# A three-layer transformer forward pass on one core: the opening norm's scales by pairs of units, its shifts as narrow matmuls

## The chip, the cores and the metric

The kernel runs on one core of a Trainium2 chip. The metric is the device time of one execution in microseconds, lower is better. The core has TensorE (PE; its weight loads are listed apart as PEld and overlap the matmuls), VectorE (DVE), ScalarE (ACT), GpSimdE (POOL), SyncE (SP, which issues nearly all DMAs) and 16 DMA engines between HBM and the on-chip memory. Engines run their own instructions strictly in order and wait for each other on semaphores.

## The reference

All arrays are float32. A first block has two layers, a second block one; the tokens are 256 rows of 1024. What the change touches is the start of layer 0 of the first block: the modulation vector, the first RMS norm and the first projection.

```python
def rms_norm(x, g):
    xf = x.astype(jnp.float32)
    y = xf * lax.rsqrt(jnp.mean(xf * xf, axis=-1, keepdims=True) + EPS)
    return (y * g.astype(jnp.float32)).astype(x.dtype)

def hybrid_layer(x, mod, norm1, norm2, w_in, ...):
    shift1, scale1, gate1, shift2, scale2, gate2 = jnp.split(mod[:, None, :], 6, axis=-1)
    h = rms_norm(x, norm1) * (1.0 + scale1) + shift1
    proj = h @ w_in
    ...

def first_block(x, c, w_mod, b_mod, ...):
    c_act = jax.nn.silu(c)
    for l in range(DEPTH):
        mod = c_act @ w_mod[l] + b_mod[l]
        x = hybrid_layer(x, mod, ...)
    return x
```

## The kernel before

**Layout.** Activations are kept transposed: 128 features on the partitions, 256 tokens along the row, eight such blocks (kc = 0 to 7) for the 1024 features. Weights come from HBM as panels of 1 MB (128 partitions x 2048 float32; 256 output columns of a 1024-row matrix, laid out by kc). To keep float32 accuracy with the fast format, each panel and each activation is split in a high and a low part: ACT copies the panel to the high part (`split_hi`, L430), DVE subtracts it from the panel to get the low part (`split_lo`, L437), and TensorE multiplies three products per block (high x high L442, high x low L443, low x high L444). A panel is 48 such matmuls of 256 columns. Raw panels live in a ring of six slots (`raw`, the low part is written over them as `ring_w`), high parts in four (`w_hi`).

**The modulation vector.** `mod` is a vector times a matrix. Its 6144 outputs per layer are 24 units of 256 outputs, 1 MB each, with the outputs on the partitions and the 1024 inputs along the row. DVE multiplies each half of a unit with the row `crow` (silu of c, spread over all partitions by TensorE transposes) and sums along the row: `dve_mod`, L1167, two instructions a unit, each with a small one that fetches the sum. In layer 0 the units 0 to 3 are shift1 and 4 to 7 are scale1. The remaining units come later, between other work, through two buffers `modw` and the semaphore `mod_used`, on which SP waits before it reloads a buffer (L367).

**The opening.** SP issues, in this order: ccol (c, norm1 and the first 16 columns of b_mod), the first part of the constants, x (1 MB), the eight units 0 to 7 (L2333), panels 0 and 1 (L362), the rest of the constants, panels 2 to 5, and then units 8, 9 and panels 6, 7 as their buffers come free. TensorE turns c (L2374) and x (L2381), ACT copies x and squares it, TensorE sums the squares (L592), and ACT takes the inverse root `rs` (L942, L943). DVE sums the eight units, adds the bias (L1176), forms the gain `gcol` = (1 + scale) x norm1 (L2417), and then per block kc: `tbuf` = x * gcol * rs (L1195), ACT adds the shift and rounds (`act_hi`, L967), DVE takes the rest (`act_lo`, L1200). Between them stand the splits of panels 0 and 1. TensorE multiplies panel 0 (`pe_head_late`): for kc 0 to 3 first the two products with the high weights (L528, L529), then those with the low weights (L533), then kc 4 to 7 as three products. Panels 1, 2, 3 follow through `pe_panel`; the small compression matmuls (`cmp`, 60 columns) are mixed into panel 3 and need `tb`, which ACT and DVE prepare from the results of panels 0 and 1 (L999 to L1017 on ACT, L1300 and L1303 on DVE). GpSimd loads the layer's constants `lc` (436 KB) once `mod_used` stands at 2 + 7.

Everything in the rest of the program is ordered by hand in each engine's own program and by semaphores; the change leaves the order there as it is.

Of the kernel before, what the change touches and what calls it, by code (L numbers as in the profile page):

```python
# [104 lines left out]
def build(nc, a, out, layers=DEPTH):  # L105
    ctx = ExitStack()

    def sb(name, shape, dt=F32):
        return ctx.enter_context(nc.sbuf_tensor(name, shape, dt))

    def sem(name):
        return ctx.enter_context(nc.semaphore(name))

    with ctx:
# [23 lines left out]
        crow = sb("crow", [P, D])  # L138
        modc = sb("modc", [P, 48])
# [38 lines left out]
        cst_more = sem("cst_more")  # L178
        gcol_ready = sem("gcol_ready")
# [16 lines left out]
        modraw_x = [sem(f"modraw_x{i}") for i in range(6)]  # L196
# [33 lines left out]
        class Chain:  # L230
# [13 lines left out]
            def end(self):  # L244
# [33 lines left out]
        first_units = [modw[:, 0, :], modw[:, 1, :], modw_x[:, 0, :], modw_x[:, 1, :],  # L278
                       *[v[:, b * PANEL:(b + 1) * PANEL] for v in (mixf, act_flat) for b in range(2)]]
# [238 lines left out]
        def pe_head_late(pe, m, k, o, arrive):  # L518


            pe.wait_ge(hi_done, rounded(m, k))
            wh, wl = w_hi[slot(k)], w_lo(m, k)
            col = lambda kc, c: slice(kc * 256 + c * P, kc * 256 + (c + 1) * P)
            row = lambda c: o[:, c * T:(c + 1) * T]
            for kc in range(4):
                arrive(kc)
                for c in range(2):
                    nc.tensor.matmul(row(c), wh[:, col(kc, c)], act_hi[:, kc, :], start=kc == 0 and c == 0, stop=False, skip_group_check=True)  # L528
                    nc.tensor.matmul(row(c), wh[:, col(kc, c)], act_lo[:, kc, :], start=False, stop=False, skip_group_check=True)  # L529
            pe.wait_ge(lo_done, rounded(m, k))  # L530
            for kc in range(4):
                for c in range(2):
                    nc.tensor.matmul(row(c), wl[:, col(kc, c)], act_hi[:, kc, :], start=False, stop=False, skip_group_check=True)  # L533
            for kc in range(4, KC):
                arrive(kc)
                for c in range(2):
                    last = mm3(row(c), wh[:, col(kc, c)], wl[:, col(kc, c)], act_hi[:, kc, :], act_lo[:, kc, :], False, kc == KC - 1, skip=True)
            return last
# [421 lines left out]
        def act_norm(act, l, q, link, shift):  # L960
            act.wait_ge(ss_done, q + 1)
            rsqrt(link, rs[:, :], bank[6][:, 0:T], 1.0 / D, cst[:, C_EPS:C_EPS + 1]).then_inc(rs_done, 1)
            if q == 0:
                split_hi(act, 0, 0)
            for kc in range(KC):
                act.wait_ge(t_done, 8 * q + kc + 1)
                nc.scalar.activation(act_hi[:, kc, :], tbuf[:, kc, :], ACT.Identity, bias=modc[:, shift + kc:shift + kc + 1])\  # L967
                    .then_inc(act_his, 1)
                if q == 0 and kc == 3:
                    split_hi(act, 0, 1)  # L970
            if q == 0:
                act_masks(act)
# [217 lines left out]
        def dve_norm(dve, q, g0, shift):  # L1190

            dve.wait_ge(rs_done, q + 1)
            for kc in range(KC + 1):
                if kc < KC:
                    nc.vector.scalar_tensor_tensor(tbuf[:, kc, :], x[:, kc, :], gcol[:, g0 + kc:g0 + kc + 1], rs[:, :], ALU.mult, ALU.mult)\  # L1195
                        .then_inc(t_done, 1)
                if kc:
                    c = kc - 1
                    dve.wait_ge(act_his, 8 * q + c + 1)
                    nc.vector.scalar_tensor_tensor(act_lo[:, c, :], tbuf[:, c, :], modc[:, shift + c:shift + c + 1],  # L1200
                                                   act_hi[:, c, :].bitcast(F32), ALU.add, ALU.subtract).then_inc(act_ready, 1)
                    if q == 0 and c == 3:
                        split_lo(dve, 0, 0)
            if q == 0:
                split_lo(dve, 0, 1)

        def dve_layer(dve, l, link, ahead):
# [83 lines left out]
            if l:  # L1291
                dve_modc(dve, modc_ready, 3 * l + 2, 64, lc[:, LC_BM:LC_BM + 8], 36)
# [70 lines left out]
            if l == 0:  # L1363
                dve_modc(dve, modc_ready, 3 * l + 2, 16, lc[:, LC_BM:LC_BM + 8], 12)
# [999 lines left out]
        def _(pe):  # L2364
            pe.sem_inc(split_free, SPLIT)
            pe.sem_inc(mod_used, 2)
# [42 lines left out]
        def _(dve):  # L2409
            link = Chain(dve, dve_links, DVE_LINKS)  # L2410
            dve.wait_ge(cact_ready, 2)
            for u in range(8):
                dve.wait_ge(modraw[u] if u < 2 else modraw_x[u - 2], 16)
                dve_mod(first_units[u], modsum, 2 * u)
            dve.wait_ge(c_loaded, 16)
            dve_modc(dve, modc_ready, 1, 0, ccol[:, 2 * KC:2 * KC + 16], 8)
            nc.vector.scalar_tensor_tensor(gcol[:, 0:KC], modc[:, 8:16], 1.0, ccol[:, KC:2 * KC], ALU.add, ALU.mult).then_inc(gcol_ready, 1)  # L2417
            dve.wait_ge(gcol_ready, 1)
# [31 lines left out]
def lay_out(i):  # L2450
# [24 lines left out]
    modw = i["w_mod"].transpose(0, 2, 1).reshape(DEPTH * MOD_PANELS, 2, P, D).transpose(0, 2, 1, 3).reshape(-1, P, PANEL)  # L2475
    w = i["w_in_2"]
# [38 lines left out]
```

## Time and profile before

| | us |
|---|---|
| median of 3 runs (1230.19 to 1238.47) | 1230.28 |
| the profiled execution | 1229.85 |
| its span, first to last instruction | 1228.1 |
| TensorE busy in it | 1166.4 (95%) |
| DVE busy | 903.4 (74%) |
| ACT busy | 609.2 (50%) |

The profiled execution took 1.75 us more than its span. TensorE's clock was granted at 0.984 of full on the mean: it has two levels, 2.4 GHz (1.00 in the rows) and 1.2 GHz (0.50). "Idle before, releaser" is how long an engine had stood still and what let it go on.

### The profile page before, as it was taken

To read this page: it belongs to the slowest core of one execution; us is meant where nothing else is said; L and a number is where in the kernel's file an instruction comes from. 1 tells how busy PE (TensorE), PEld (TensorE's weight loads), DVE (VectorE), ACT (ScalarE), POOL (GpSimd) and SP (SyncE) were. 2 spreads that over 40 slices of the span, in tenths; PEclk is the share of its full clock that TensorE was granted. 3 is DMA by queue.
4 is the path that set the end of the run, shared out by engine and by line. 5 is a ranking of instruction groups with operands and counts; after the bars stand their busy time and mean duration, and the time that the engine had idled before them with its cause. 6 is when DMAs were issued, how large, how long until landed. Compare 5 with 4: busy or idle time off the path is not lost.

```text
span 1228.1 us, 19648 instructions
## 1 busy us (share of the span) xinstructions
PE 1166.4 (95%) x7990; PEld 1058.5 (86%) x7990; DVE 903.4 (74%) x1201; ACT 609.2 (50%) x811; POOL 58.5 (5%) x61
## 2 busy tenths in 40 slices
PE   3999999999989999999999999999999998999996
PEld 2978989999988888999999989988878997888885
DVE  6889798877788976855568369986785857656555
ACT  3753354444465435444444435557788733444441
POOL 1017000000000520000000000000000000000000
PEclk7899999999999999999999999999999999999999
DMA  9845467868765416455566534454784564555540
GB/s 379 348 170 206 169 244 282 301 244 300 276 230 231 168 52 238 172 193 184 179 248 215 175 134 138 140 193 161 245 292 138 189 219 141 171 188 190 196 146 34
DMA packets 44058, 249.34 MB, mean 203 GB/s; under 512 B 4352, under 2 KB 12672, under 8 KB 15952
## 3 DMA queue, kind: packets, MB, share of 16 engines
q1 hardware_dynamic: 43568, 246.19, 55.8%
q0 software_dynamic: 416, 2.11, 0.5%
q8 instruction: 53, 0.87, 0.3%
q14 instruction: 21, 0.17, 0.1%
HBM read 247.17 MB, written 1.11 MB: 202 GB/s over the span
## 4 chain that ended last, share of the span: by engine, by line
PE 82%; DVE 8%; ACT 5%; DMA 2%; issue 1%; SPq 0%; POOL 0%; DVEq 0%; ACTq 0%; POOLq 0%
PE bank L442 17%; PE bank L443 16%; PE bank L444 16%; PE bank L799 14%; PE bank L802 7%; PE bank L882 2%; DMA raw<-in_panels 2%; PE bank L923 1%; DVE ring_w L437 1%; ACT mixf L1953 1%; PE bank L1725 1%; PE bank L1843 1%; PE bank L781 1%; ACT mixf L1954 1%; DMA arena<-in_modw 1%
## 5 line engine op out<-in xcount | busy, mean ns | idle before, releaser
L437 DVE TENSOR_TENSOR ring_w<-raw,w_hi 128x2048 fp32r<-128x2048 f32 x166 | 381.4, 2301 | 138.8 <-ACT w_hi L430 138.5
L430 ACT ACTIVATE w_hi<-raw 128x2048 fp32r<-128x2048 f32 x166 | 316.3, 1909 | 165.3 <-PE bank L444 152.6
L442 PE MATMUL bank<-act,w_hi 128*128 128x256 f32 x728 | 211.7, 291 | 6.4 <-DVE act L1200 2.7
L443 PE MATMUL bank<-act,w_hi 128*128 128x256 f32 x728 | 206.4, 284 | 0.0
L444 PE MATMUL bank<-act,ring_w 128*128 128x256 f32 x728 | 206.3, 283 | 0.0
L799 PE MATMUL bank<-act,w_hi 128*128 128x512 f32 x736 | 184.7, 393 | 0.2 <-DVE act L2280 0.2
L443 PE MATMUL bank<-ff_lo,w_hi 128*128 128x256 f32 (+1 forms) x560 | 158.2, 283 | 0.0
L444 PE MATMUL bank<-ff_hi,ring_w 128*128 128x256 f32 (+1 forms) x560 | 158.2, 282 | 0.0
L442 PE MATMUL bank<-ff_hi,w_hi 128*128 128x256 f32 (+1 forms) x560 | 157.7, 282 | 0.0
L799 PEld LDWEIGHTS bank<-act,w_hi 128*128 128x128 f32 x736 | 133.8, 189 | 25.3 <-issue 0.6
L442 PEld LDWEIGHTS bank<-act,w_hi 128*128 128x128 f32 x728 | 140.1, 192 | 13.0 <-issue 10.0
L443 PEld LDWEIGHTS bank<-act,w_hi 128*128 128x128 f32 x728 | 140.1, 192 | 0.1
L444 PEld LDWEIGHTS bank<-act,ring_w 128*128 128x128 f32 x728 | 140.0, 192 | 0.0
L1167 DVE CUSTOM_DVE_ANT_0 arena<-arena,crow 128x1024 f32<-128x1024 f32 x88 | 106.0, 1243 | 10.8 <-DMA arena<-in_modw 10.6
L1127 ACT ACTIVATE arena<-bank 128x256 f32<-128x256 f32 x96 | 36.6, 383 | 152.8 <-PE bank L802 149.1
L443 PEld LDWEIGHTS bank<-ff_lo,w_hi 128*128 128x128 f32 x560 | 107.5, 192 | 0.0
L442 PEld LDWEIGHTS bank<-ff_hi,w_hi 128*128 128x128 f32 x560 | 107.5, 192 | 0.0
L444 PEld LDWEIGHTS bank<-ff_hi,ring_w 128*128 128x128 f32 x560 | 107.5, 192 | 0.0
L802 PEld LDWEIGHTS bank<-act,ring_w 128*128 128x128 f32 x736 | 100.4, 190 | 7.2
L802 PE MATMUL bank<-act,ring_w 128*128 128x256 f32 x736 | 102.6, 282 | 0.0
L1459 DVE TENSOR_TENSOR arena<-bank,arena 128x256 f32<-128x256 f32 x96 | 39.8, 421 | 63.3 <-ACT arena L1127 63.2
L442 PE MATMUL bank<-mix_hi,w_hi 128*128 128x256 f32 x192 | 55.4, 289 | 0.0
(347 smaller groups left out, 1887.3 us busy)
## 6 DMA issues: line engine op xcount, KB each, us to landing
raw<-in_panels SPq DMA_DIRECT2D x170, 1024.0 KB, 4.8
arena<-in_modw SPq DMA_DIRECT2D x44, 1024.0 KB, 7.2
mixf<-dscr SPq DMA_DIRECT2D x8, 512.0 KB, 5.2
arena<-dscr SPq DMA_DIRECT2D x8, 512.0 KB, 4.9
mixf<-in_modw SPq DMA_DIRECT2D x2, 1024.0 KB, 16.3
act_flat<-in_modw SPq DMA_DIRECT2D x2, 1024.0 KB, 20.0
mixf<-dscr SPq DMA_DIRECT2D x8, 256.0 KB, 6.7
arena<-dscr SPq DMA_DIRECT2D x8, 256.0 KB, 5.9
```

The source lines that it names most:

```text
L430: nc.scalar.activation(w_hi[slot(k)][:, :], w_raw(m, k), ACT.Copy).then_inc(hi_done, 1)
L437: nc.vector.tensor_tensor(w_lo(m, k), w_raw(m, k), w_hi[slot(k)][:, :].bitcast(F32), ALU.subtract).then_inc(lo_done, 1)
L442: nc.tensor.matmul(o, wh, xh, start=start, stop=False, skip_group_check=skip)
L443: nc.tensor.matmul(o, wh, xl, start=False, stop=False, skip_group_check=skip)
L444: return nc.tensor.matmul(o, wl, xh, start=False, stop=stop, skip_group_check=skip)
L781: nc.tensor.matmul(bank[c][:, :], wh[:, s:s + P], act2[:, kc, :, :], start=kc == 0, stop=False, skip_group_check=True)
L799: nc.tensor.matmul(bank[4 + c][:, :], wh[:, s:s + P], act2[:, kc, :, :], start=kc == 0, stop=False)
L802: last = nc.tensor.matmul(bank[4 + c][:, 0:T], wl[:, s:s + P], act_hi[:, kc, :], start=False, stop=kc == KC - 1)
L882: mm = lambda o, w, x, first=False, last=False: nc.tensor.matmul(o, w, x, start=first, stop=last, skip_group_check=True)
L1127: nc.scalar.activation(fr[par][:, c * T:(c + 1) * T], up_bank(at, c, final)[:, T:2 * T], ACT.Copy).then_inc(ff_cross, 1)
L1167: last = nc.vector.tensor_tensor_reduce(o, o, crow[:, :], 1.0, 0.0, ALU.mult, ALU.add, sums[:, col + b:col + b + 1])
L1459: nc.vector.tensor_tensor(fr[par][:, c * T:(c + 1) * T], up_bank(at, c, final)[:, 0:T], fr[par][:, c * T:(c + 1) * T], ALU.add).then_inc(f ...
```

## The change

The order of the opening's loads changes: scale and shift units alternate (4, 0, 5, 1), then panel 0, then 6, 2, 7, 3, then panel 1. The first two lie in the raw ring's slots 4 and 5, so that panels 4 and 5 are loaded only when those units are used. DVE sums only the four scale units. The four shift units are laid out in HBM like a weight panel, and TensorE multiplies them with `scol` (silu of c as eight columns, an extra small ACT instruction): `pe_shift`, 16 matmuls of one moving column a unit. The norm is done in pairs of blocks in a new DVE program `dve_open`. `pe_head_late` is gone; layer 0 uses `pe_head`, which wants panel 0's high and low parts and has the fourth `pe_shift` in it ahead of kc 2. GpSimd's load of `lc` keeps its number, but the count now starts at 2 + 4, so that it goes after the third scale unit.

```diff
+        scale_units = [raw[:, 4, :], modw[:, 0, :], modw_x[:, 0, :], mixf[:, 0:PANEL]]
+        shift_units = [raw[:, 5, :], modw[:, 1, :], modw_x[:, 1, :], mixf[:, PANEL:2 * PANEL]]
-        def pe_head_late(pe, m, k, o, arrive):
...
+        def pe_shift(pe, u):
+            pe.wait_ge(shift_raw[u], 16)
+            for c in range(2):
+                for kc in range(KC):
+                    s = kc * 256 + c * P
+                    last = nc.tensor.matmul(bank[u][:, c:c + 1], shift_units[u][:, s:s + P], scol[:, kc:kc + 1], start=kc == 0, stop=kc == KC - 1)
+            last.then_inc(shift_sums, 1)
...
             def arrive(kc):
+                if l == 0 and kc == 2:
+                    pe_shift(pe, 3)
                 pe.wait_ge(act_ready, 16 * l + kc + 1)
...
-                    last = (pe_head if l else pe_head_late)(pe, m, k, G(g), arrive)
+                    last = pe_head(pe, m, k, G(g), arrive)
...
-            if q == 0:
-                split_hi(act, 0, 0)
             for kc in range(KC):
+                if q == 0:
+                    act.wait_ge(modc_ready, kc // 2 + 1)
                 act.wait_ge(t_done, 8 * q + kc + 1)
...
-                if q == 0 and kc == 3:
-                    split_hi(act, 0, 1)
+                if q == 0 and kc in (1, 5):
+                    split_hi(act, 0, kc // 4)
...
+            def scale_sum(j):
+                dve.wait_ge(scale_raw[j], 16)
+                dve_mod(scale_units[j], modsum, 8 + 2 * j)
...
+            def shift(j):
+                dve.wait_ge(shift_sums, j + 1)
+                nc.vector.tensor_tensor(modc[:, 2 * j:2 * j + 2], bank[j][:, 0:2], ccol[:, 2 * KC + 2 * j:2 * KC + 2 * j + 2], ALU.add).then_inc(modc_ready, 1)
...
+            scale_sum(0)
+            scale_sum(1)
+            gain(0, 2, 0)
+            dve.wait_ge(rs_done, 1)
+            scaled(0, 1, 2, 3)
+            shift(0)
+            low(0, 1)
+            split_lo(dve, 0, 0)
+            shift(1)
+            scale_sum(2)
+            low(2, 3)
+            gain(2, 3, 1)
+            scaled(4, 5)
+            shift(2)
+            scale_sum(3)
+            low(4, 5)
+            gain(3, 4, 2)
+            scaled(6, 7)
+            shift(3)
+            low(6, 7)
+            split_lo(dve, 0, 1)
...
-            for u in range(8):
-                sp.dma_start(first_units[u], a["modw"][u]).then_inc(modraw[u] if u < 2 else modraw_x[u - 2], 16)
-            load(sp, 0, 0)
+            for j in range(4):
+                sp.dma_start(scale_units[j], a["modw"][4 + j]).then_inc(scale_raw[j], 16)
+                sp.dma_start(shift_units[j], a["modw"][j]).then_inc(shift_raw[j], 16)
+                if j == 1:
+                    load(sp, 0, 0)
             load(sp, 0, 1)
...
+            sp.wait_ge(mod_used, 2 + 4 + 1)
+            load(sp, 0, 4)
+            sp.wait_ge(shift_sums, 2)
+            load(sp, 0, 5)
...
             pe_norm_sum(pe, 0)
+            pe.wait_ge(cact_ready, 3)
+            for u in range(3):
+                pe_shift(pe, u)
```

TensorE's instructions from the sum of squares to the first matmuls of panel 0, before:

```order
L592 MATMUL bank<-arena,cst 128x256 [waits sq_done] x8
L528 MATMUL bank<-act,w_hi 128x256 [waits hi_done,act_ready,gfree0,cact_ready]
L529 MATMUL bank<-act,w_hi 128x256
L528 MATMUL bank<-act,w_hi 128x256
L529 MATMUL bank<-act,w_hi 128x256
L528 MATMUL bank<-act,w_hi 128x256 [waits act_ready]
```

The same place after the change (L582 is the sum of squares, L527 is `pe_shift`, L444 to L446 are the three products):

```order
L582 MATMUL bank<-arena,cst 128x256 [waits sq_done] x8
L527 MATMUL bank<-scol,raw 128x1 [waits shift_raw0,cact_ready]
L527 MATMUL bank<-scol,raw 128x1 x15
L527 MATMUL bank<-scol,arena 128x1 [waits modraw1]
L527 MATMUL bank<-scol,arena 128x1 x15
L527 MATMUL bank<-scol,arena 128x1 [waits shift_raw2]
L527 MATMUL bank<-scol,arena 128x1 x15
L444 MATMUL bank<-act,w_hi 128x256 [waits lo_done,act_ready,gfree0,cact_ready]
L445 MATMUL bank<-act,w_hi 128x256
```

Three `pe_shift` (48 matmuls) now stand between the sum of squares and panel 0; the fourth stands behind the first 12 matmuls of panel 0. ACT's opening before, from the inverse root on:

```order
L943 ACTIVATE rs<-rs 128x256 [waits act_links]
L430 ACTIVATE w_hi<-raw 128x2048 [waits split_free,raw_ready0]
L967 ACTIVATE act<-arena,modc 128x256 [waits t_done] x4
L430 ACTIVATE w_hi<-raw 128x2048 [waits split_free,raw_ready1]
L967 ACTIVATE act<-arena,modc 128x256 [waits t_done] x4
```

The same after (L935 is the root's end, L959 the rounded activations, L432 the high parts of panels):

```order
L935 ACTIVATE rs<-rs 128x256 [waits act_links]
L959 ACTIVATE act<-arena,modc 128x256 [waits t_done,modc_ready] x2
L432 ACTIVATE w_hi<-raw 128x2048 [waits split_free,raw_ready0]
L959 ACTIVATE act<-arena,modc 128x256 [waits t_done,modc_ready] x4
L432 ACTIVATE w_hi<-raw 128x2048 [waits split_free,raw_ready1]
L959 ACTIVATE act<-arena,modc 128x256 [waits t_done,modc_ready] x2
```

Panel 0's high part moved behind the first two blocks, panel 1's behind the first six.

## Rows read from the trace of the kernel before

**Rows 1.** The page, part 1: busy time, share of the span and instructions.

```profile
PE 1166.4 (95%) x7990; PEld 1058.5 (86%) x7990; DVE 903.4 (74%) x1201; ACT 609.2 (50%) x811; POOL 58.5 (5%) x61
```

**Rows 2.** Windows: length, busy time (instructions) per engine, granted clock, DMA share, GB/s.

```profile
15.00:20.00 5.00, 1.07 (x5) 0.59 (x4) 4.81 (x9) 1.05 (x3) 0.00 (x0) 0.83 1.01 428
20.00:25.00 5.00, 0.00 (x0) 0.00 (x0) 4.79 (x9) 0.00 (x0) 0.00 (x0) 0.50 1.01 428
...
35.00:40.00 5.00, 4.27 (x20) 3.97 (x20) 4.82 (x8) 3.35 (x8) 0.00 (x0) 0.50 1.01 419
...
45.00:50.00 5.00, 5.00 (x44) 5.00 (x43) 3.97 (x3) 4.00 (x8) 0.00 (x0) 1.00 1.01 421
50.00:60.00 10.00, 10.00 (x88) 10.00 (x86) 8.32 (x11) 6.58 (x8) 0.00 (x0) 1.00 0.56 202
```

**Rows 3.** The chain that ended last: start, length, what it was.

```profile
6.71 22.91 DMA raw<-in_panels
...
29.64 1.91 ACT w_hi L430
...
34.85 2.21 DVE ring_w L437
...
37.10 2.07 PE bank L533 x8
39.17 0.21 PE bank L442
...
42.97 0.12 PE bank L444
```

**Rows 4.** Timeline of DVE: first unit's sum, third unit's, panel 1's low part.

```profile
10.02 1.23 DVE L1167 CUSTOM_DVE_ANT_0 arena<-arena,crow 128x1024 f32<-128x1024 f32 x1 [10.02 <-DMA arena<-in_modw]
...
14.76 1.23 DVE L1167 CUSTOM_DVE_ANT_0 arena<-arena,crow 128x1024 f32<-128x1024 f32 x1
...
40.01 2.28 DVE L437 TENSOR_TENSOR ring_w<-raw,w_hi 128x2048 fp32r<-128x2048 f32 x1
```

**Rows 5.** Timeline around TensorE's gap, and the first matmul of panel 1.

```profile
12.35 3.72 PE L592 MATMUL bank<-arena,cst 128*128 128x256 f32 x16 [1.26 <-ACT arena L2400]
...
16.11 0.47 ACT L942 ACTIVATE rs<-bank,cst 128x256 f32<-128x256 f32 x1 [0.95 <-PE bank L592]
...
32.62 0.55 PE L528 MATMUL bank<-act,w_hi 128*128 128x256 f32 x1 [16.54 <-DVE act L1200]
...
43.28 0.28 PE L442 MATMUL bank<-act,w_hi 128*128 128x256 f32 x1
```

**Rows 6.** Timeline of the narrowest plain float32 matmuls (15 columns), weight loads.

```profile
81.62 0.30 PEld L691 LDWEIGHTS bank<-sqc,cst 128*128 128x128 f32 x2 [0.67 <-ACT arena L1072]
...
81.84 0.30 PEld L692 LDWEIGHTS bank<-small,cst 128*128 128x128 f32 x2
...
82.06 0.19 PEld L442 LDWEIGHTS bank<-act,w_hi 128*128 128x128 f32 x1
```

**Rows 7.** Groups by shape, weight loads, 0 to 120 us: busy us, mean ns.

```profile
L528 PEld LDWEIGHTS bank<-act,w_hi 128*128 128x128 f32 x8 | 2.6, 325 | 16.9 <-issue 16.9
...
L691 PEld LDWEIGHTS bank<-sqc,cst 128*128 128x128 f32 x2 | 0.3, 188 | 0.7 <-ACT arena L1072 0.7
```

**Rows 8.** Windows of 1 us where the granted clock falls, and where it rises.

```profile
17.00:18.00 1.00, 0.00 (x0) 0.00 (x0) 0.93 (x3) 0.03 (x1) 0.00 (x0) 1.00 1.00 426
18.00:19.00 1.00, 0.00 (x0) 0.00 (x0) 1.00 (x3) 0.00 (x0) 0.00 (x0) 0.67 1.07 451
...
42.00:43.00 1.00, 1.00 (x9) 1.00 (x9) 0.74 (x2) 1.00 (x2) 0.00 (x0) 0.89 1.04 434
```

**Rows 9.** Timeline of ACT and DVE behind panels 0 and 1.

```profile
44.22 0.36 ACT L999 ACTIVATE arena<-bank 128x256 f32<-128x256 f32 x1
...
49.24 0.39 ACT L1008 ACTIVATE arena<-bank 128x256 f32<-128x256 f32 x1 [0.94 <-PE bank L444]
...
53.38 1.16 DVE L1303 TENSOR_TENSOR ff_lo<-arena,ff_hi 128x960 fp32r<-128x960 f32 x1 [1.05 <-ACT ff_hi L1017]
```

More of the change, by code:

```diff
@@ L138, in build @@
         crow = sb("crow", [P, D])
+        scol = sb("scol", [P, KC])
         modc = sb("modc", [P, 48])
@@ L195, in build @@
         modraw = [sem(f"modraw{i}") for i in range(2)]
-        modraw_x = [sem(f"modraw_x{i}") for i in range(6)]
+        scale_raw, shift_raw = [[sem(f"{n}_raw{i}") if i != 1 else modraw[b] for i in range(4)] for b, n in enumerate(("scale", "shift"))]
         mod_used = sem("mod_used")
@@ L516, in pe_head @@
             return last
-        def pe_head_late(pe, m, k, o, arrive):
[L521 to L538, printed above, removed]
+        def pe_shift(pe, u):
[5 more added lines that the diff above has]
+            last.then_inc(shift_sums, 1)
         def pe_panel_rows(pe, m, k, o, xh, xl, first, last_panel, parts=False):
@@ L1201, in dve_norm, with dve_open, gain, scaled @@
                                                    act_hi[:, c, :].bitcast(F32), ALU.add, ALU.subtract).then_inc(act_ready, 1)
[L1202 to L1205, printed above, removed]
+        def dve_open(dve):
+            def scale_sum(j):
+                dve.wait_ge(scale_raw[j], 16)
+                dve_mod(scale_units[j], modsum, 8 + 2 * j)
+            def gain(a, b, n):
+                dve.wait_ge(mod_used, 2 + 4 + b)
+                v = slice(2 * a, 2 * b)
+                sc = slice(8 + 2 * a, 8 + 2 * b)
+                nc.vector.tensor_tensor(modc[:, sc], modsum[:, sc], ccol[:, 2 * KC + 8 + 2 * a:2 * KC + 8 + 2 * b], ALU.add).then_inc(gcol_ready, 1)
+                dve.wait_ge(gcol_ready, 2 * n + 1)
+                nc.vector.scalar_tensor_tensor(gcol[:, v], modc[:, sc], 1.0, ccol[:, KC + 2 * a:KC + 2 * b], ALU.add, ALU.mult).then_inc(gcol_ready, 1)
+                dve.wait_ge(gcol_ready, 2 * n + 2)
+            def scaled(*kcs):
+                for kc in kcs:
+                    nc.vector.scalar_tensor_tensor(tbuf[:, kc, :], x[:, kc, :], gcol[:, kc:kc + 1], rs[:, :], ALU.mult, ALU.mult).then_inc(t_done, 1)
+            def shift(j):
+                dve.wait_ge(shift_sums, j + 1)
+                nc.vector.tensor_tensor(modc[:, 2 * j:2 * j + 2], bank[j][:, 0:2], ccol[:, 2 * KC + 2 * j:2 * KC + 2 * j + 2], ALU.add).then_inc(modc_ready, 1)
+            def low(*kcs):
+                for kc in kcs:
+                    dve.wait_ge(modc_ready, kc // 2 + 1)
+                    dve.wait_ge(act_his, kc + 1)
+                    nc.vector.scalar_tensor_tensor(act_lo[:, kc, :], tbuf[:, kc, :], modc[:, kc:kc + 1], act_hi[:, kc, :].bitcast(F32), ALU.add, ALU.subtract)\
+                        .then_inc(act_ready, 1)
+            dve.wait_ge(c_loaded, 16)
+            scale_sum(0)
[19 more added lines that the diff above has]
+            split_lo(dve, 0, 1)
@@ L2394, in _ @@
                 nc.scalar.activation(crow[:, 512 * n:512 * (n + 1)], bank[4 + n][:, :], ACT.Silu).then_inc(cact_ready, 1)
+            act.wait_ge(c_loaded, 16)
+            nc.scalar.activation(scol[:, :], ccol[:, 0:KC], ACT.Silu).then_inc(cact_ready, 1)
             for j in range(4):
@@ L2411, in _ @@
             dve.wait_ge(cact_ready, 2)
[L2412 to L2418, printed above, removed]
             for l in range(layers):
@@ L2475, in lay_out @@
     modw = i["w_mod"].transpose(0, 2, 1).reshape(DEPTH * MOD_PANELS, 2, P, D).transpose(0, 2, 1, 3).reshape(-1, P, PANEL)
+    modw[:4] = [col_panel(i["w_mod"][0], slice(256 * u, 256 * (u + 1))) for u in range(4)]
     w = i["w_in_2"]
```

23 lines of the change are left out of this document (12 added, 11 removed).

## The prediction

> **What bounds the kernel now.** I read the busy times first: TensorE is busy 95% of the span [rows 1], so the time is TensorE's work plus the places where it stands still. Then the windows of the opening: the largest such place is here. From 16.1 us (end of the sum of squares, 12.35 + 3.72) to 32.62 TensorE does nothing, 16.54 us [rows 5], while the DMA engines are full (428 GB/s) and DVE is busy 4.8 of 5 us [rows 2]. The chain says who ends last: the landing of panel 0 at 29.6, its high part on ACT, the alternation of L1195 and L1200 on DVE, panel 0's low part (34.85, 2.21 us), and from 37.10 TensorE itself [rows 3]. After that TensorE has no gap: 10.00 of 10 us busy in 50 to 60 [rows 2], and panel 1 begins at 43.28 [rows 5] although its low part was there at 42.29 (40.01 + 2.28) [rows 4]. So whatever brings panel 1 forward, with the work behind it, is gained. The other thing to see is the clock: it falls at about 18.3 (0.67 in 18 to 19), when TensorE has stood still for two us, and returns at about 42.2 (0.89 in 42 to 43) [rows 8]. All of panel 0 but its last matmuls is multiplied at 1.2 GHz, 0.21 us a matmul instead of 0.12 [rows 3].
>
> **Part by part: the loads.** One megabyte takes (29.62 − 10.02)/8 = 2.45 us [rows 3, 4], and the DMA engines are full until about 50 in either order [rows 2]. The number of bytes ahead of panel 1 is the same. In the new order I put the landings at: scale 0 10.0, shift 0 12.5, scale 1 14.9, shift 1 17.4, panel 0 19.8, scale 2 22.3, shift 2 24.7, scale 3 27.2, shift 3 29.6, panel 1 32.1. The new waits of SP (first scale unit used, two shift units done) stand ahead of panels 4 and 5, which land after 40, and of units 8 and 9 and panels 6 and 7 behind them in the same queue; they end by 12.4 and by 20 to 28, with three to six loads still queued in the engines. I cost them at nothing; the cover is gone only if the second shift unit ends after about 38. The load of lc goes at about 27.6 as before.
>
> **DVE.** Four units leave: they are 4 x 2.37 = 9.5 us of work (two units in 14.76 − 10.02) [rows 4], but DVE was paced by the loads, so this counts only through the order. DVE now: scale 0 to 12.4, scale 1 to 17.3, gain (two small instructions) 17.7, four scaled blocks 19.4, shift 0, two low blocks (ACT between) 21.3, panel 0's low part behind its high part (19.8 or 20.8 + 1.9): 22.7 to 25.0. Then shift 1, scale 2 27.6, two low blocks 28.5, gain and two scaled blocks 29.8, shift 2 30.0, scale 3 32.4, two low blocks 33.3, gain and two scaled 34.6, shift 3 34.8. ACT takes panel 1's high part from 32.1 to 34.0 and the last two blocks to 35.8; DVE's last low blocks end at 36.2 and panel 1's low part at 36.2 + 2.3 = **38.5**. That is DVE's price, if no shift comes late.
>
> **TensorE's new work, the term that decides.** A shift unit is 16 matmuls of one column. No row has that shape. The nearest are the plain float32 matmuls of 15 columns: each makes two weight loads and two passes, and starts 0.22 us after the one before (81.62, 81.84, 82.06) [rows 6]. A unit is so 16 x 0.22 = 3.5 us at 2.4 GHz. From below it is bounded by one load per matmul, 16 x 0.12 = 1.9 us. From above by 1.2 GHz: the weight load is 325 ns on the mean there against 188 [rows 7], and the pace of loads with matmuls is 0.21 [rows 3], so 32 x 0.21 = 6.7 us. With 3.5: shift 0 16.1 to 19.6, shift 1 to 23.1, shift 2 24.7 to 28.2, blocks 0 and 1 of panel 0 (12 x 0.12) to 29.6, shift 3 to 33.2, blocks 2 and 3 34.6, blocks 4 and 5 36.1, blocks 6 and 7 (ready at 36.2) about 37.0. TensorE then waits for panel 1 until 38.5.
>
> **The sum.** Panel 1 starts at 38.5 instead of 43.28: −4.8 us. What is late next: the compression matmuls in panel 3, which need tb. Before, DVE finished it at 54.5 (53.38 + 1.16) [rows 9], and TensorE came there at 43.28 + 2 x 5.8 + 1.8 = 56.7, so 2.2 us of slack. Now ACT is the busier: the high parts of panels 2 and 3 wait for their landings (about 37.2 and 39.7, lc's load included), so the copies of panel 0's result (44.22 before [rows 9]) start at 41.6 and not 5 us earlier; I follow this to a tb at about 51.3 against TensorE's 51.9. It just holds; I take 0.3 us off for it. The rest of the layer is started by TensorE's results and moves along. So −4.5: the profiled execution would go from 1229.85 to 1225.4, and the median, 0.43 above it, from 1230.28 to **1225.8**.
>
> A rule to weigh: rows 6 show 0.22 us for a narrow float32 matmul, which is two weight loads. The Trainium skill, page "TensorE: Matmul & The Clock Gate", section "Wait — 56ns, not 53.3ns?", says that the start-to-start time of matmuls never drops below about 25 ns however small they are, which leaves the weights out. By that alone a unit would cost 16 x 25 ns = 0.4 us, an estimate from the page. The gain would still be DVE's 38.5, and rival A would be gone; the row speaks against it and decides.
>
> **Rival A, slower: the clock does not count these matmuls.** The fall at 18.3 came in a stretch in which TensorE was busy to 16.1 and then idle [rows 5, 8]. If 64 matmuls of one column, nearly all weight load, are to the clock what standing still is, it falls at 18.3 as before and the units are multiplied at 1.2 GHz. Then shift 0 ends at 20.7, shift 1 27.5, shift 2 34.3, blocks 0 and 1 at 36.9, shift 3 43.7, and the last 36 matmuls start there, at 0.21 us until the clock returns, to about 50. Panel 1 starts at 50 instead of 43.3: +6.7, 1237.0. The point from which the change is a loss: 16.1 + 4u + 48p = 43.3, with p = 0.21 for the matmuls u = 4.2 us a unit, with p = 0.12 u = 5.4; 3.5 lies below both, 6.7 above both. For A: no row has so narrow matmuls in a long stretch; the narrowest long ones (60 columns at the compression, inside 50 to 60 and on) share it with 256-column ones. Against: the engine is occupied without a gap, and its fall needed real standing still.
>
> **Rival B: a dip.** The units count, but the gap between shift 1 and shift 2 (23.1 to 24.7) or the phase of the clock lets it fall at about 25. Shift 2 then takes to 31.4, the clock is back soon after, blocks 0 and 1 to 33, shift 3 36.5, the rest 40.8: −2.5, 1227.8.
>
> **Rival C: the gain is taken back.** Panel 1 starts early, but tb misses TensorE by more than a few tenths or the sums of units 8 to 10 on DVE, which start only some 3 us earlier, reach into what TensorE waits for. Each such wait could take 1 to 4 us: 1229, no change.
>
> **Chances.** Forecast 0.50; A 0.31; B 0.11; C 0.08. I prefer the forecast to A because TensorE has no gap in its instructions, though no row proves that this is what counts. Low end: the forecast with panel 1 at 37.5 (a cheaper unit cannot give more than DVE allows) and no loss at tb, 1224.2. High end: A with its late return of the clock, 1238. Both signs hold much of the chance, so beside the whole range 1224.2 to 1238 the forecast's own is 1224.2 to 1227. One per cent is 12.3 us, about what a measurement of this kernel can tell from no change; no case reaches that: faster 0.01, same 0.96, slower 0.03 (A with a second delay behind it).
>
> **What would show it.** TensorE's L527: 2 records per matmul, 64 matmuls, 14 us in all at 1.00 (forecast) or 27 us at 0.50 (A). The granted clock between 18 and 36: 1.00, or 0.50 as before. Panel 1's first matmul at 38.5 (forecast), 41 (B), 50 (A). DVE's L1217 idle before it: near nothing, or until a late L527 (A). The compression's first matmul with no idle before it. The prediction fails if the units cost otherwise than 3.5 us, if panel 0 does not land at about 20, or if the work behind panel 1 does not move by the same amount.

## The result, and the profile after

The changed kernel takes 1235.89 us (median of 20 runs, 1234.11 to 1243.44) against 1230.14 us before (20 runs, 1227.85 to 1238.47): a ratio of 1.0057, interval 1.0048 to 1.0067. (The ratios here and below are those on record, not the quotients of the two medians; that would be 1.0047 here.) It is slower by half a per cent, which is within 1% but well outside what the runs scatter. The forecast was 1225.8; what came is rival A, which I had put at 1237.0 with a chance of 0.31. The profiled execution has a span of 1233.5 us, and took 1235.25.

Part 1 of the page of the changed kernel, to be read beside [rows 1]:

```profile
PE 1188.3 (96%) x8118; PEld 1081.4 (88%) x8118; DVE 894.9 (73%) x1193; ACT 609.2 (49%) x812; POOL 58.5 (5%) x61
```

TensorE has 128 more records (64 matmuls, two each) and is busy 21.9 us more; DVE has 8.5 us less. The span grew by 5.4. So TensorE has taken over more time than DVE gave up, and the next thing to ask is where. I matched the same instruction in both traces, counted from the end of the program, and took the difference of their starts: +5.42 to +5.49 from 49.5 to 147 us, +5.48 at 600, +5.37 at the end. The whole loss is made before panel 1 and is there again at the end. (In between the difference stands at +7.0 for a while: each trace has one later fall of the clock that the other lacks, at 938 us in the changed kernel and at 1012 us before, and they cancel.) Windows of the opening of the changed kernel (columns as in [rows 2]):

```profile
15.00:20.00 5.00, 5.00 (x47) 4.97 (x45) 4.25 (x12) 1.88 (x5) 0.00 (x0) 1.00 1.02 424
20.00:25.00 5.00, 4.28 (x22) 4.20 (x21) 3.48 (x5) 2.21 (x3) 0.00 (x0) 0.51 1.01 416
...
30.00:35.00 5.00, 5.00 (x25) 5.00 (x25) 2.34 (x4) 1.71 (x3) 0.00 (x0) 0.50 1.01 413
...
45.00:50.00 5.00, 5.00 (x34) 5.00 (x34) 4.82 (x3) 3.96 (x6) 0.00 (x0) 0.76 0.87 320
```

Before, DVE was the full engine from 15 to 25 and TensorE stood still [rows 2]. Now it is the other way round: TensorE is full but for one wait of 1.35 us, and DVE works 2.34 of 5 us in 30 to 35. But look at the eighth number, the granted clock: 1.00 in the first window and 0.51 in the second, with TensorE occupied without a gap in the first and well into the second. Windows of 1 us show the moment:

```profile
19.00:20.00 1.00, 1.00 (x11) 1.00 (x11) 0.37 (x1) 0.98 (x3) 0.00 (x0) 1.00 1.04 434
20.00:21.00 1.00, 1.00 (x8) 1.00 (x7) 0.51 (x2) 1.00 (x1) 0.00 (x0) 0.55 1.01 418
21.00:22.00 1.00, 1.00 (x6) 1.00 (x6) 0.24 (x1) 0.72 (x1) 0.00 (x0) 0.50 1.05 426
```

Before, the fall at 18.3 came after two us of standing still [rows 8]. Here the busy time is 1.00 of 1.00 on both sides of the fall, and what TensorE does there is the second shift unit. The timeline of the changed kernel gives the four units, the DVE instruction that takes each up, and panel 1:

```profile
15.15 3.63 PE L527 MATMUL bank<-scol,raw 128*128 128x1 f32 x32
18.64 5.65 PE L527 MATMUL bank<-scol,arena 128*128 128x1 f32 x32
...
25.64 6.99 PE L527 MATMUL bank<-scol,arena 128*128 128x1 f32 x32 [1.35 <-DMA arena<-in_modw]
32.66 0.16 DVE L1217 TENSOR_TENSOR modc<-bank,ccol 128x2 f32<-128x2 f32 x1 [3.92 <-PE bank L527]
...
35.19 6.82 PE L527 MATMUL bank<-scol,mixf 128*128 128x1 f32 x32
42.05 0.16 DVE L1217 TENSOR_TENSOR modc<-bank,ccol 128x2 f32<-128x2 f32 x1 [4.96 <-PE bank L527]
...
43.65 2.28 DVE L439 TENSOR_TENSOR ring_w<-raw,w_hi 128x2048 fp32r<-128x2048 f32 x1
...
48.71 0.28 PE L444 MATMUL bank<-act,w_hi 128*128 128x256 f32 x1
```

The same 16 matmuls take 3.63 us at 1.00, 5.65 with the fall inside, and 6.99 and 6.82 at 0.50. DVE, which was to set the pace, now waits 3.92 and 4.96 us for them. Panel 1's first matmul comes at 48.71, against 43.28 [rows 5]. One line by its tiles shows why a unit doubles. These are the weight loads of L527: count, shortest, median and longest in ns, then first and last start:

```profile
L527 PEld LDWEIGHTS bank<-scol,raw x32: 190/192/192, 14.9 to 18.5; 128*128 128x128 f32 x32
...
L527 PEld LDWEIGHTS bank<-scol,mixf x32: 330/333/333, 35.0 to 41.6; 128*128 128x128 f32 x32
```

A matmul of one column has two weight loads, and 32 loads in 3.63 us are 0.113 us each: the loads set its pace, and they go with the clock. The chain that ended last goes through nothing else until panel 1:

```profile
5.45 20.15 DMA arena<-in_modw
25.64 6.99 PE bank L527 x32
...
35.39 6.62 PE bank L527 x32
42.01 0.42 PE bank L444
```

The landing of shift 2, its 16 matmuls, the first blocks of panel 0, shift 3's 16 matmuls, the rest of panel 0: all of it on TensorE, at half clock until 47.4. In [rows 3] this stretch belonged to a DMA, ACT and DVE.

### The profile page after: what moved, and what is told of

Its sections match the earlier page's. It is cut to its first block, busy times and chain, and to the rows that moved or that the text cites. A ratio compares the mean times of both kernels' runs of the same rounds, so it can differ in the third digit from the quotient of the medians.

```text
span 1233.5 us, 19913 instructions
## 1 busy us (share of the span) xinstructions
PE 1188.3 (96%) x8118; PEld 1081.4 (88%) x8118; DVE 894.9 (73%) x1193; ACT 609.2 (49%) x812; POOL 58.5 (5%) x61
## 4 chain that ended last, share of the span: by engine, by line
PE 83%; DVE 8%; ACT 5%; DMA 2%; issue 1%; SPq 0%; POOL 0%; DVEq 0%; ACTq 0%; POOLq 0%
PE bank L444 17%; PE bank L445 16%; PE bank L446 16%; PE bank L791 14%; PE bank L794 7%; PE bank L874 2%; DMA arena<-in_modw 2%; PE bank L915 1%; PE bank L527 1%; ACT mixf L1997 1%; DVE ring_w L439 1%; PE bank L1769 1%; PE bank L1887 1%; PE bank L773 1%; ACT mixf L1998 1%
## 5 line engine op out<-in xcount | busy, mean ns | idle before, releaser
L432 ACT ACTIVATE w_hi<-raw 128x2048 fp32r<-128x2048 f32 x166 | 316.4, 1910 | 151.5 <-PE bank L446 151.0
L444 PE MATMUL bank<-act,w_hi 128*128 128x256 f32 x736 | 216.1, 294 | 6.0 <-DVE act L1192 2.7
L445 PE MATMUL bank<-act,w_hi 128*128 128x256 f32 x736 | 210.3, 286 | 0.0
L446 PE MATMUL bank<-act,ring_w 128*128 128x256 f32 x736 | 210.3, 286 | 0.0
L446 PE MATMUL bank<-ff_hi,ring_w 128*128 128x256 f32 (+1 forms) x560 | 158.2, 283 | 0.0
L444 PE MATMUL bank<-ff_hi,w_hi 128*128 128x256 f32 (+1 forms) x560 | 157.7, 282 | 0.0
L791 PEld LDWEIGHTS bank<-act,w_hi 128*128 128x128 f32 x736 | 133.7, 189 | 25.2 <-issue 0.6
L444 PEld LDWEIGHTS bank<-act,w_hi 128*128 128x128 f32 x736 | 143.4, 195 | 12.6 <-issue 10.0
L445 PEld LDWEIGHTS bank<-act,w_hi 128*128 128x128 f32 x736 | 143.5, 195 | 0.1
L446 PEld LDWEIGHTS bank<-act,ring_w 128*128 128x128 f32 x736 | 143.2, 195 | 0.0
L444 PEld LDWEIGHTS bank<-ff_hi,w_hi 128*128 128x128 f32 x560 | 107.5, 192 | 0.0
L446 PEld LDWEIGHTS bank<-ff_hi,ring_w 128*128 128x128 f32 x560 | 107.5, 192 | 0.0
L794 PEld LDWEIGHTS bank<-act,ring_w 128*128 128x128 f32 x736 | 100.4, 190 | 7.2
L1159 DVE CUSTOM_DVE_ANT_0 arena<-arena,crow 128x1024 f32<-128x1024 f32 x84 | 101.3, 1243 | 3.3 <-DMA arena<-in_modw 3.1
L794 PE MATMUL bank<-act,ring_w 128*128 128x256 f32 x736 | 102.6, 282 | 0.0
L444 PE MATMUL bank<-mix_hi,w_hi 128*128 128x256 f32 x192 | 55.4, 289 | 0.0
## 6 DMA issues: line engine op xcount, KB each, us to landing
mixf<-in_modw SPq DMA_DIRECT2D x2, 1024.0 KB, 23.1
```

What stands on the lines that cost most here:

```text
L432: nc.scalar.activation(w_hi[slot(k)][:, :], w_raw(m, k), ACT.Copy).then_inc(hi_done, 1)
L444: nc.tensor.matmul(o, wh, xh, start=start, stop=False, skip_group_check=skip)
L445: nc.tensor.matmul(o, wh, xl, start=False, stop=False, skip_group_check=skip)
L446: return nc.tensor.matmul(o, wl, xh, start=False, stop=stop, skip_group_check=skip)
L791: nc.tensor.matmul(bank[4 + c][:, :], wh[:, s:s + P], act2[:, kc, :, :], start=kc == 0, stop=False)
L794: last = nc.tensor.matmul(bank[4 + c][:, 0:T], wl[:, s:s + P], act_hi[:, kc, :], start=False, stop=kc == KC - 1)
```

## Theories

**T1: width.** One-column matmuls do not hold the granted clock, whatever their number; the unit then costs 6.9 us instead of 3.5 and is above the break-even of 4.2 to 5.4 that the prediction worked out. With the clock held, panel 1 should come at about 38.5.

**T2: occupation or phase.** The clock follows how TensorE is occupied (a gap, or a moment that the new order shifts), and width has no part in it.

**T3: order.** The new order of sums, blocks and parts on DVE and ACT costs the time by itself, with or without TensorE's new work.

## Experiment 1: the same matmuls, 128 columns wide

To the changed kernel: the one column of the moving operand is read 128 times over, so that each matmul is as wide as a tile, with the same weights, the same count and the same place.

```diff
-  last = nc.tensor.matmul(bank[u][:, c:c + 1], ..., scol[:, kc:kc + 1], ...)
+  last = nc.tensor.matmul(bank[u][:, c * 128:(c + 1) * 128], ..., scol[:, kc:kc + 1].to_broadcast([P, 128]), ...)
-  nc.vector.tensor_tensor(modc[...], bank[j][:, 0:2], ...)
+  nc.vector.tensor_tensor(modc[...], bank[j][:, 0:256:128], ...)
```

> The changed kernel with each of the 64 shift matmuls given 128 moving columns instead of one (the same column of c repeated; the results are the same, DVE reads one column of each). The number of matmuls and weight loads is unchanged. Theory (T1, rival A of the prediction): TensorE was without a gap from 14.9 us, yet its clock fell to 0.50 at 20.1 us in the second shift unit, because one-column matmuls do not hold the clock; with wide ones it stays at 1.00, a unit takes 3.5 us instead of 6.9, panel 1's first matmul starts at about 38.5 us and the kernel takes about 1225.8 us, 0.9965 of before. Rival (T2): the clock fell at that moment whatever runs; then nothing changes, units of 6.9 us, 1236 us. Rival (T3): the loss comes from the new order on DVE and ACT and not from TensorE; then the clock stays up but panel 1 still starts at 45 us or later, 1232 us or more.

Measured: 1228.18 us (11 runs) against 1229.98, ratio 0.9999 (0.9979 to 1.0019). Windows of this kernel's opening:

```profile
15.00:20.00 5.00, 5.00 (x36) 4.69 (x34) 3.52 (x10) 0.89 (x2) 0.00 (x0) 1.00 1.02 423
20.00:25.00 5.00, 5.00 (x47) 5.00 (x46) 2.25 (x5) 2.71 (x3) 0.00 (x0) 1.00 1.01 418
```

and its timeline:

```profile
17.21 3.73 PE L527 MATMUL bank<-scol,raw 128*128 128x128 f32 x32
...
20.78 7.31 PE L527 MATMUL bank<-scol,arena 128*128 128x128 f32 x64
...
30.23 3.84 PE L527 MATMUL bank<-scol,mixf 128*128 128x128 f32 x32 [0.70 <-DMA mixf<-in_modw]
...
36.39 2.29 DVE L439 TENSOR_TENSOR ring_w<-raw,w_hi 128x2048 fp32r<-128x2048 f32 x1
...
38.83 0.35 PE L444 MATMUL bank<-act,w_hi 128*128 128x256 f32 x1 [0.45 <-DVE ring_w L439]
```

Where one column had 0.51, 128 columns have 1.00. The width costs nothing: 3.73 us a unit beside 3.63, since the weight loads set the pace. Panel 1 starts at 38.83, held by its low part on DVE (36.39 + 2.29), as the prediction had it at 38.5. That is 4.45 us earlier than before, of which some 0.6 need not be the change's: x landed at 6.76 us in this execution and at 7.37 before, and the units' loads stand behind it. T1 holds. Against T2 this trace alone is not proof. The edit changes nothing but the width (and DVE's stride in the bank), and the 1.35 us gap of the changed kernel comes after its fall. But the two executions differ in one thing more: the clock rose to 1.00 at 9.85 us in the changed kernel and at 15.64 here, so that the sum of squares was slower and shift 0 began 2.1 us later. Experiments 9 and 10 separate the two. The ratio is still no gain that a measurement can tell, and the 1225.8 us expected are 2.4 us off. The profiled run's own gain was 4.33 us at 147 and 4.17 at 353. Then this window took 1.1 of them:

```profile
350.00:355.00 5.00, 5.00 (x30) 5.00 (x31) 4.82 (x13) 3.43 (x8) 0.00 (x0) 0.66 0.91 381
```

There the clock fell at 350.14 for 3.4 us, which it did not do in the trace of before. The slow stretch lies on full work, but the fall came just behind a wait:

```profile
349.87 0.36 PE L444 MATMUL bank<-act,w_hi 128*128 128x256 f32 x1 [2.69 <-DVE act L1192]
```

The same wait of 2.69 us is in every trace, and not all have the fall. At the end 2.9 us of 4.45 are left. Eight of the 11 runs lie at 1226 to 1229.2, with a mean granted clock of 0.990 to 0.994, and three at 1235, with 0.985 or 0.986. Later falls of the clock make a spread as large as what the opening gives; for the runs without a trace that is read from the mean clock only.

## Experiments 2 and 5: 32 and 64 columns

The edit of experiment 1 with 32, then 64 in place of 128.

> The same with 32 moving columns instead of 128. T1 leaves open how wide they must be: either the clock falls near 20 us as with one column (about 1236 us), or it holds (about 1226 us). The price of a unit at 1.00 should be 3.5 us either way, since the weight loads pace it. T2: as with one column. T3: 1232 us or more.

> The changed kernel with 64 moving columns in each shift matmul; one column and 32 lost the clock in the second shift unit, 128 kept it at 1.00. T1 alone doesn't say which side 64 falls on: with the clock kept panel 1 starts at about 38.6 us and the kernel is at 0.996 to 1.000 of before, as with 128; with the clock lost at 48.6 and 1.0065. If the clock were lost for a reason that has nothing to do with width (T2), 64 would be as one column.

Measured for 32: 1237.18 (6 runs), ratio 1.0065 (1.0043 to 1.0087). For 64: 1229.59 (10 runs) against 1231.05, ratio 0.9991 (0.997 to 1.0012). The window from 20 to 25 of the two, first 32 columns:

```profile
20.00:25.00 5.00, 3.62 (x25) 3.49 (x24) 3.75 (x5) 2.57 (x4) 0.00 (x0) 0.66 1.01 415
...
455.00:460.00 5.00, 5.00 (x24) 4.78 (x23) 2.45 (x5) 0.00 (x0) 0.00 (x0) 0.50 0.01 2
```

and 64 columns:

```profile
20.00:25.00 5.00, 4.99 (x45) 4.86 (x45) 2.31 (x5) 2.71 (x3) 0.00 (x0) 1.00 1.02 418
```

32 columns behave like one (the fall comes at 21.6, and panel 1's work is 4.81 us late), 64 like 128 (panel 1 at 38.81, its work 4.05 us early; a fall at 350 then takes 1.2 us here too). No more is known than that these four widths fall on two sides in this place; and 32 columns had the clock early (from 11.35 us), 64 late (from 15.45), so these two differ in more than width. The second line of 32 columns is from a long fall late in that profiled run, from 451.7 to 465.3, which cost 6.1 us by itself. It is most of why that run took 1244.28 and its median is only 1237.18.

## Experiment 3: the new order without the new matmuls

All eight first units are summed on DVE in the order of their landing; the shift units come in the other units' layout, and TensorE gets no L527.

```diff
-  pe_shift(pe, u)            # all four
+  def shift_sum(j):          # on DVE, called where unit j lands
+      dve.wait_ge(shift_raw[j], 16)
+      dve_mod(shift_units[j], modsum, 2 * j, shift_sums)
```

> One part of the change alone: the new order of loads and the norm by pairs, but all eight units summed on DVE (in the order of their landing), none on TensorE. T1 says that the DVE work of 8 x 2.37 us plus the norm now stands in one line: I add it up to panel 1's low part at about 44.4 us against 42.3 before, and TensorE's clock is at 0.50 until a few us later, so about +1 to +4 us over before, 1231 to 1234. If T3 were right, it would be at least as slow as the changed kernel, 1236 us.

Measured: 1232.44 (10 runs; ratio 1.0024, 1.0006 to 1.0041). One execution of 2313 us is in this median and not in the ratio; the other nine have 1232.3. Timeline:

```profile
41.66 2.29 DVE L439 TENSOR_TENSOR ring_w<-raw,w_hi 128x2048 fp32r<-128x2048 f32 x1
...
44.10 0.36 PE L444 MATMUL bank<-act,w_hi 128*128 128x256 f32 x1 [0.60 <-DVE ring_w L439]
```

Panel 1 comes 0.82 us later than before. So the order by itself gives nothing and takes little: T3 cannot explain 5.4 us. It also says that the 4.45 us of experiment 1 are not to be had from the new order alone: they need the four sums taken off DVE. The rest of the profiled run's loss (3.5 at the end) is two clock falls, 1.4 us at 83.3 and 1.15 at 356.4. Time and low part (43.95) are as expected.

## Experiments 4 and 8: the kernel before, its gap filled wide and narrow

To the kernel before: 36 matmuls into a bank that nobody reads, between the sum of squares and panel 0, 256 columns wide in experiment 4 and one column wide in experiment 8.

```diff
+  for n in range(36):
+      nc.tensor.matmul(bank[7][:, 0:T], ones, x[:, n % KC, :], start=True, stop=True)       # 4
+      nc.tensor.matmul(bank[7][:, 0:1], ones, x[:, n % KC, 0:1], start=True, stop=True)     # 8, in its place
```

> The kernel before with 36 matmuls of 256 columns (results unused, in a bank that is free) put into TensorE's gap between 16.1 and 32.6 us, so that its clock stays at 1.00. It shows what the clock alone was worth in the kernel before. Theory: panel 0 is then held up by DVE and not by TensorE, and panel 1 starts when its low part is there, 42.3 us instead of 43.28: -1.0 us, 1229.1. Rival: each of the 40 slow matmuls counts, -4 us, 1226.

> The kernel before with 36 matmuls of ONE column (plain float32, results unused) in TensorE's gap from 16.1 us; the run with 36 matmuls of 256 columns in that place held the clock at 1.00 up to 34 us. T1: one-column matmuls are to the clock like standing still, so it falls near 18 to 20 us although TensorE is occupied to about 31, and the kernel takes what it took before, 1230 us (ratio 1.000). T2 (the clock follows whether the engine is occupied): it stays at 1.00 as with the wide ones.

Measured for 4: 1232.36 (10 runs), ratio 1.0029 (1.0008 to 1.005); for 8: 1232.1 (10 runs) against 1229.63, ratio 1.0014 (1.0001 to 1.0026). The timeline and a window of experiment 4:

```profile
15.25 15.70 PE L2385 MATMUL bank<-x,cst 128*128 128x256 f32 x72
...
40.56 2.29 DVE L437 TENSOR_TENSOR ring_w<-raw,w_hi 128x2048 fp32r<-128x2048 f32 x1
43.00 0.34 PE L442 MATMUL bank<-act,w_hi 128*128 128x256 f32 x1
...
20.00:25.00 5.00, 5.00 (x25) 4.40 (x24) 4.81 (x9) 0.00 (x0) 0.00 (x0) 1.00 1.02 428
```

and the same of experiment 8:

```profile
15.15 10.67 PE L2385 MATMUL bank<-x,cst 128*128 128x1 f32 x72
...
20.00:25.00 5.00, 5.00 (x27) 5.00 (x27) 3.87 (x8) 0.00 (x0) 0.00 (x0) 0.53 1.02 426
```

This is the cleanest pair: in a kernel without any of the change, TensorE is busy 5.00 of 5.00 us in both, and the clock is 1.00 under wide matmuls and 0.53 under narrow ones (it falls at 20.3). Being occupied is not what counts. The pair says a second thing, which speaks against reading T1 as a gain in itself: a faster panel 0 brings almost nothing here. In experiment 4 the clock fell at 34.08, so that panel 0 was slow after all; it ended together with DVE's low part (40.56 + 2.29 = 42.85), and panel 1 begins at 43.00, 0.28 earlier than before. In experiment 8 the clock was back at 37.4, and TensorE was done early and waited for DVE:

```profile
42.94 0.36 PE L442 MATMUL bank<-act,w_hi 128*128 128x256 f32 x1 [1.25 <-DVE ring_w L437]
```

In this kernel DVE's low part is the bound, and what TensorE gains is hidden behind it; the clock decides only where TensorE has been given the work. Neither kernel reached its expectation (1229.1 or 1226 for 4, 1230 for 8), for both profiled runs lose some 2.5 us later. 1.5 go in a clock fall at about 82, and another 1.5 and 1.2 at 154 to 160 (a few tenths come back after each), where a modulation unit lands later and DVE waits 2.00 and 1.71 us for it against 0.56 before. The load of that unit took 8.4 and 8.1 us from its issue instead of 6.9; why is not settled.

## Experiment 7: two of everything, at full clock

The 128 columns of experiment 1, every matmul of the shift units made twice.

```diff
-  for c in range(2):
+  for c in (0, 1, 0, 1):
```

> 128 moving columns and each shift unit multiplied twice (the second time over the first, same result): 32 matmuls a unit, 7.0 us at the full clock, which is what 16 cost at half clock. It tells apart what the lost clock took: the price of the units (then panel 1 starts late although the clock is at 1.00) or the slow multiplication of panel 0. By the prediction's formula 16.1 + 4u + 48p with u = 7.0 and p = 0.12 panel 0 ends at about 49 us against 48.6 in the changed kernel: +5 to +6 us over before, 1235.5. Rival: the units are largely hidden behind the loads and DVE, and panel 1 starts before 44 us, 1231 or less.

Measured: 1239.79 (4 runs), ratio 1.0072 (1.0058 to 1.0087), 4 us more than expected. The clock is 1.00 throughout the opening, and panel 1 is 8.50 us later than before:

```profile
40.32 7.31 PE L527 MATMUL bank<-scol,mixf 128*128 128x128 f32 x64
...
51.78 0.29 PE L444 MATMUL bank<-act,w_hi 128*128 128x256 f32 x1
...
30.00:35.00 5.00, 5.00 (x48) 5.00 (x47) 3.08 (x8) 0.91 (x2) 0.00 (x0) 1.00 1.01 418
```

A unit of 7.2 us at full clock loses as the unit of 6.9 at half clock does. The prediction's formula holds with the start that the trace has (17.2 instead of 16.1): 17.2 + 4 x 7.2 + 48 x 0.12 = 51.8, measured 51.78. That start is one part of what was over the expectation, which also has 49 us where the formula with its own 16.1 and 7.0 gives 49.9. Behind panel 1 the profiled run lost another 2.5 us, nearly all in two clock falls at 90.6 and 363.7. So the price of the four units (and of panel 0's 48 matmuls) is enough to explain the loss, whatever makes it dear.

## Experiment 6: an attempt to do better

Experiment 1 with the third scale sum moved ahead of panel 0's low part, since DVE has time there.

```diff
   low(0, 1)
+  scale_sum(2)
   split_lo(dve, 0, 0)
   shift(1)
-  scale_sum(2)
-  low(2, 3)
   gain(2, 3, 1)
+  low(2, 3)
```

> 128 moving columns, and in DVE's opening the sum of the third scale unit stands ahead of panel 0's low part (and the third gain ahead of the low blocks 2 and 3). In the run with 128 columns DVE stood idle 1.24 us before that low part, waiting for ACT, while the third scale unit had landed. Theory: with the clock kept the opening is bound by DVE, so what DVE gains there reaches panel 1 until the fourth shift unit's end (34.1 us) is late: panel 1 at 37.8 to 38.4 us instead of 38.6, the kernel 0.2 to 0.8 us faster than with 128 columns alone, about 1227.5. Rival: TensorE needs panel 0's low part sooner than DVE has it in this order, and nothing or less is gained.

Measured: 1228.01 (12 runs) against 1231.05, ratio 0.9989 (0.9973 to 1.0004). Panel 1 came 1.4 us later than in experiment 1, not earlier; some 0.6 of it may be this execution's own, whose x landed at 7.36 us and not at 6.76:

```profile
26.30 0.70 POOL L2408 DMA_DIRECT2D lc<-in_lcs  x1 [22.05 <-DVE modsum L1159]
...
34.54 1.92 ACT L432 ACTIVATE w_hi<-raw 128x2048 fp32r<-128x2048 f32 x1 [3.29 <-DMA raw<-in_panels]
...
40.19 0.36 PE L444 MATMUL bank<-act,w_hi 128*128 128x256 f32 x1 [0.81 <-DVE ring_w L439]
```

GpSimd's load of lc (436 KB) waits for that sum. It went out at 26.30 instead of 29.24 (experiment 1), into the same full DMA engines, and panel 1 landed later: its high part begins at 34.54, there at 32.69. Experiment 10 lies between them in both, lc at 28.03 and the high part at 33.76. Experiments 3 and 5 fit as well: lc at 29.92 and 29.23, panel 1 landed at 32.35 and 33.01, against 34.51 here. That order fits this reading; no kernel moved lc alone. My expectation failed because I had moved the sum and not asked who waits for it.

## Experiments 9 and 10: the changed kernel and the 128 columns again

Both unchanged, on one chip beside experiment 8.

> The changed kernel without an edit, for a second profile and a direct comparison: the clock falls in the second shift unit again (19 to 23 us), four units of 3.5 to 6.9 us, panel 1's low part from 43 to 44 us, 1.005 to 1.007 of before.

> The changed kernel with 128 columns once more, since its first interval (0.9979 to 1.0019) held three runs near 1235 us among eight near 1227: if its opening is 4.3 us shorter, as the trace shows, and 1.1 us are lost when the clock falls near 350 us, the bulk should be at 1226 to 1229 us, 0.997 to 0.999 of before.

Measured against 1229.63 us before: the changed kernel 1234.43 (5 runs), ratio 1.0047 (1.0032 to 1.0062); with 128 columns 1227.04 (12 runs), ratio 0.9986 (0.9976 to 0.9996). A window of experiment 9, then:

```profile
20.00:25.00 5.00, 5.00 (x33) 5.00 (x33) 2.55 (x4) 2.71 (x3) 0.00 (x0) 0.68 1.01 416
```

and, of experiment 10, the same window, the third shift unit, panel 1's start and the window in which experiment 1 had lost the clock:

```profile
20.00:25.00 5.00, 3.30 (x30) 3.11 (x28) 3.18 (x5) 2.67 (x3) 0.00 (x0) 1.00 1.01 418
...
25.73 3.84 PE L527 MATMUL bank<-scol,arena 128*128 128x128 f32 x32 [2.43 <-DMA arena<-in_modw]
...
39.40 0.35 PE L444 MATMUL bank<-act,w_hi 128*128 128x256 f32 x1 [0.52 <-DVE ring_w L439]
...
350.00:355.00 5.00, 4.87 (x37) 4.82 (x38) 4.82 (x13) 3.18 (x7) 0.00 (x0) 1.00 0.97 406
```

The first repeats the result: the fall comes at 21.8 with TensorE busy 5.00 of 5.00, and the work from panel 1 on is 4.82 us late (its profiled run has a further long fall, 134.5 to 148.1, for 6.2 us). The second had no fall at 350, and its 3.9 us at panel 1 arrive at the end as 3.8.

The two settle what experiment 1 left open of T2. The clock rose early (9.85 and 11.04 us) in the changed kernel and in experiment 10, late (15.01 and 15.64) in experiments 9 and 1. Whether early or late, it fell under one column and held under 128. And in experiment 10 it held although TensorE stood still 2.43 us and was busy only 3.30 of 5 us, where experiment 9, busy 5.00 of 5, lost it.

With 128 columns the kernel is clearly faster than the changed one, by 0.6%. Against the kernel before it is open: 0.14% faster here, with an interval that ends just below 1, and an interval around 1 in experiment 1.

## Why the prediction was wrong

**The step that failed** is in the prediction's part on TensorE's new work: "A unit is so 16 x 0.22 = 3.5 us at 2.4 GHz", with the choice behind it, "I prefer the forecast to A because TensorE has no gap in its instructions". The price at 2.4 GHz was right (3.63 measured), and so was the one at 1.2 GHz (6.7 estimated, 6.82 to 6.99 measured). What was wrong was the reason for choosing between them. The prediction said that no row proved that a gap is what counts, and still gave it 0.50. Experiments 4 and 8 show that it is not: no gap around 20 us in either, and two clocks. In the changed kernel the clock fell at 20.1 us, in the middle of unbroken work, and three of the four units ran wholly or partly at 1.2 GHz: 23.1 us in all instead of 14.

**Rival A** has the course of it. Its ends of the units were 20.7, 27.5, 34.3 and 43.7 us; measured 18.8, 24.3, 32.6 and 42.0, panel 1 at 48.7 instead of 50. The difference is in two things: the sum of squares ended earlier (shift 0 begins at 14.93, not 16.1), and the clock fell at 20.1, not 18.3, so that the first unit was done at full clock. The loss was then 5.4 instead of 6.7.

**The rule of the Trainium skill** ("TensorE: Matmul & The Clock Gate", section "Wait — 56ns, not 53.3ns?", a floor of about 25 ns between starts) was set aside for rows 6, and the trace bears the rows out: 3.63 us for 16 matmuls is 0.227 us each, at full clock.

**DVE's price**, 38.5, was right where TensorE was not late: 38.83 and 39.40 in experiments 1 and 10. It is no bound of the changed kernel, whose DVE waits.

**The break-even**, a unit of 4.2 to 5.4 us, fits what was measured: 3.7 gained (experiment 1), 6.9 and 7.2 lost (the changed kernel, experiment 7). No kernel lay between, so its place is not shown more closely.

**The loads.** SP's new waits cost nothing that shows in the opening, in any of the kernels. The lc load was taken as fixed at 27.6; it went at 29.24 in experiment 1, and experiment 6 suggests that its moment moves panel 1. In the changed kernel, with lc at 27.45, panel 1 landed at 34.18 and not at 32.1; that was hidden behind TensorE.

**What is late next.** The 0.3 us put down for tb did not appear: 4.33 to 4.37 us of 4.45 were there at 68 to 147, and in experiment 10 all but a tenth. Rival C's own mechanism was not seen. That gains shrink later came of single clock falls, which the prediction did not name.

**Rival B**, a dip in the gap between shift 1 and 2, falls: the clock fell before that gap, and in experiment 10 it held over a wait of 2.43 us in just that place.

**What stays open**: why the clock falls in single places later in the program (350, 360, 82, once for 13 us) in some executions and not in others of the same kernel, and the later landing at 154 to 160 in experiments 4 and 8. The traces do show what TensorE did before: it had just stood still, 2.7 us before the falls at 350 to 366, and 0.9 and 0.5 us before those at 82 to 91. Before the falls at 20.1 to 21.8 in the opening of the changed kernel and of experiments 2, 8 and 9 it had worked without a break since 11.6 to 11.9. Of the difference between experiments 1 and 10, medians of 1228.18 and 1227.04, the falls at 350 explain what the two traces show; for the runs without a trace it is only argued, from their mean clock.

## What to carry to other kernels

When work is moved to TensorE into a place where it stood still, price it at both clocks, and find the break-even; if it lies between the two prices, try the moved matmuls wide before anything else, and read the granted clock in the trace. Where weight loads set the pace, width can be nearly free, and a column read many times over will do (3.73 us with 128 columns beside 3.63 with one for a unit here). The gain on the kernel before may still be small: here 0.14% at best. And before moving a sum, list who waits for it, the transfers of other queues too.

## What the hardware showed that I had not expected

The granted clock fell from 2.4 to 1.2 GHz while TensorE was occupied all the time: at 20.1 and 21.8 us (one column), 21.6 (32 columns) and 20.3 (one column, in the kernel before). At 64 and 128 columns in the same place, and at 256 in the kernel before, it stayed at 2.4.

The weight load follows the clock: 192 ns at 2.4 GHz, 333 ns at 1.2 GHz, so that 16 one-column matmuls take 3.63 or 6.99 us.

A single fall of 3.4 us costs 1.1 to 1.6 us, and a long one (13.6 us, 451.7 to 465.3 in experiment 2) 6.1 us. The runs of one kernel sort by it: of the changed kernel's 20, the fastest eleven are at a mean granted clock of 0.983 or 0.984 (1234.1 to 1236.1), and the slowest three at 0.976 (1242.9 to 1243.4).
